# Triangular inverses in a hybrid encoder: 8 by 8 blocks solved on VectorE in place of the first three doubling levels, and a new order of the pieces around them

## The reference, cut to what matters

```python
a_mat = jnp.where(strict, einsum('bnhid,bnhjd->bnhij', kb, kc) * decay, 0.0)
unit_lower = a_mat + jnp.eye(C)
u = solve(unit_lower, vb)                      # DeltaNet, 8 heads of 128
# RWKV-7, 8 heads of 64, token by token:
sa = einsum('bhij,bhj->bhi', state, a_t)
state = state * w_t[:, :, None, :] + sa[..., None] * b_t[:, :, None, :] + v_t[..., None] * k_t[:, :, None, :]
y = einsum('bhij,bhj->bhi', state, r_t)
```

## Time and profile before

| | us |
|---|---|
| median of 3 runs | 2767.75 (2765.85 to 2768.54) |
| the profiled execution, its own time | 2771.26 |
| its span | 2769.4 |
| TensorE busy in the span | 2725.2 (98%) |
| VectorE busy | 1542.8 (56%) |
| ScalarE busy | 1312.0 (47%) |
| GpSimd busy | 119.9 (4%) |
| TensorE's mean granted clock, share of full speed | 0.997 |

### The profile page before, as it was taken

The page is one execution under the profiler, slowest core; times in us unless marked ns, Lnnn a source line. Parts: engine busy times, 40 slices in busy tenths (PEclk is TensorE's granted clock), DMA queues, the critical chain, the costliest instruction groups (busy, mean ns, idle before and its releaser), DMA issues.

```text
span 2769.4 us, 44546 instructions
## 1 busy us (share of the span) xinstructions
PE 2725.2 (98%) x18174; PEld 2393.0 (86%) x18174; DVE 1542.8 (56%) x2048; ACT 1312.0 (47%) x1798; POOL 119.9 (4%) x167
## 2 busy tenths in 40 slices
PE   8999999999999999999999999999999999999999
PEld 8999998888888888888898997888888888888887
DVE  5655466666555555555544665666665555455454
ACT  4544444555544535445444354335555444354453
POOL 0000043000000000000000000530000000000000
PEclk9999999999999999999999999999999999999999
DMA  7454500543555555555545562004445545555553
GB/s 281 181 184 159 182 33 32 213 172 143 184 201 184 190 191 189 190 183 186 193 175 201 188 220 95 2 2 160 175 140 195 192 173 197 183 191 191 183 194 140
DMA packets 67801, 461.71 MB, mean 167 GB/s; under 512 B 7023, under 2 KB 10223, under 8 KB 13084
## 3 DMA queue, kind: packets, MB, share of 16 engines
q1 hardware_dynamic: 63824, 449.47, 45.3%
q10 hardware_dynamic: 3500, 5.21, 0.6%
q0 software_dynamic: 288, 4.19, 0.4%
HBM read 456.73 MB, written 5.27 MB: 167 GB/s over the span
## 4 chain that ended last, share of the span: by engine, by line
PE 94%; DVE 3%; ACT 2%; issue 1%; DMA 0%; POOL 0%; DVEq 0%; ACTq 0%; POOLq 0%
PE bank L423 17%; PE bank L402 13%; PE bank L404 13%; PE bank L403 13%; PE bank L425 9%; PE bank L446 6%; PE bank L448 6%; PE bank L447 6%; PE bank L1199 1%; PE bank L1172 1%; PE bank L337 1%; PE bank L2477 1%; PE bank L561 0%; PE bank L505 0%; DVE split_lo L353 0%
## 5 line engine op out<-in xcount | busy, mean ns | idle before, releaser
L353 DVE TENSOR_TENSOR split_lo<-raw,split_hi 128x1024 fp32r<-128x1024 f32 x840 | 1019.9, 1224 | 943.1 <-ACT split_hi L346 942.7
L346 ACT ACTIVATE split_hi<-raw 128x1024 fp32r<-128x1024 f32 x840 | 881.4, 1059 | 1137.6 <-PE bank L404 554.9
L423 PE MATMUL bank<-hT,split_hi 128*128 128x512 f32 x2048 | 720.8, 397 | 5.4 <-issue 5.3
L425 PE MATMUL bank<-hT,split_lo 128*128 128x256 f32 x2048 | 574.4, 280 | 0.0
L423 PEld LDWEIGHTS bank<-hT,split_hi 128*128 128x128 f32 x2048 | 385.0, 188 | 93.4 <-DVE split_lo L353 1.1
L402 PE MATMUL bank<-split_hi,u_hi 128*128 128x512 f32 x1152 | 449.8, 390 | 0.0
L404 PE MATMUL bank<-split_hi,u_lo 128*128 128x512 f32 x1152 | 448.5, 389 | 0.0
L403 PE MATMUL bank<-split_lo,u_hi 128*128 128x512 f32 x1152 | 448.4, 389 | 0.0
L425 PEld LDWEIGHTS bank<-hT,split_lo 128*128 128x128 f32 x2048 | 387.4, 189 | 5.7 <-issue 5.6
L446 PE MATMUL bank<-hT,split_hi 128*128 128x256 f32 x1328 | 376.8, 284 | 0.0
L448 PE MATMUL bank<-hT,split_lo 128*128 128x256 f32 x1328 | 375.8, 283 | 0.0
(11 more groups left out here) (471 smaller groups left out, 2266.4 us busy)
## 6 DMA issues: line engine op xcount, KB each, us to landing
raw<-in_stream SPq DMA_DIRECT2D x420, 1024.0 KB, 4.8
work<-in_mem POOLq DMA_DIRECT2D x2, 2048.0 KB, 8.5
bias_rows<-bias_line SPq DMA_DIRECT2D x1, 3072.0 KB, 12.9
x<-in_x SPq DMA_DIRECT2D x1, 2048.0 KB, 9.0
out<-x SPq DMA_DIRECT2D x4, 512.0 KB, 4.9
mwork<-bias_rows ACTq DMA_DIRECT2D x1, 1536.0 KB, 11.2
work<-bias_rows ACTq DMA_DIRECT2D x1, 1536.0 KB, 10.1
rwork<-in_wide ACTq DMA_DIRECT2D x1, 1280.0 KB, 5.9
```

The lines of the kernel that those rows point to most:

```text
L346: nc.scalar.activation(split_hi[:, u % SPLIT], raw[:, b % RAW, (u % 2) * UNIT:(u % 2 + 1) * UNIT], ACT.Copy).then_inc(s_hi, 1)
L353: nc.vector.tensor_tensor(split_lo[:, u % SPLIT], raw[:, b % RAW, (u % 2) * UNIT:(u % 2 + 1) * UNIT], f32(split_hi[:, u % SPLIT]), SUB).th ...
L423: nc.tensor.matmul(out[:, :], lhsT=w_hi[:, cols], rhs=hT[:, k].rearrange("p two s -> p (two s)"), start=k == 0, stop=False)
L425: m = nc.tensor.matmul(out[:, S:2 * S], lhsT=w_lo[:, cols], rhs=hT_hi[:, k, :], start=False, stop=k == KD - 1)
```

## The change

Levels 0 to 2 go (`BASE` = 3, `TINY` = 8). The 8x8 diagonal blocks are instead inverted by forward substitution on VectorE, all at once along the free axis:

```diff
+        def dve_inv_blocks(dve, group, views, d):
+            T, Tt = views[0][:, d], views[1][:, d]
+            if group >= 2 and d == 0:
+                dve.wait_ge(iv_f, group - 1)
+            dve.wait_ge(iv_a, 2 * group + d + 1)
+            own = const[:, C["blocks"]].unsqueeze(1).broadcast_to([P, 4, HALF])
+            dve_step(nc.vector.tensor_tensor(Tt, iv_diag[:, d], own, MULT))
+            dve_step(nc.vector.reduce_sum(tiny[:, 0, d], blocks_of(Tt).rearrange("p m b c -> p m c b"), AX_X))
...
+            nc.vector.tensor_tensor(blocks_of(T), got.broadcast_to(shape), unit.broadcast_to(shape), MULT).then_inc(iv_blk, 1)
+
+        def pe_inv_around(pe, group, views):
+            pe.wait_ge(iv_blk, 2 * group + 2)
+            if group < 4:
+                pe.wait_ge(s_eg, 2 * group + 2)
+            nc.tensor.matmul(rep_bank(group)[:, :], lhsT=const[:, C["around"]],
+                             rhs=views[0].rearrange("p d m n -> p (d m n)"), start=True, stop=True).then_inc(iv_rep, 1)
+
+        def dve_inv_solve(dve, group, views):
...
+            dve.wait_ge(iv_rep, group + 1)
+            nc.vector.tensor_copy(row[:, :, 0:1], unit[:, :, 0:1])
+            dve_step(nc.vector.scalar_tensor_tensor(out=row[:, :, 1:], in0=N[:, :, 0, 1:], scalar=const[:, C["unit_neg"]],
+                                                    in1=unit[:, :, 1:], op0=MULT, op1=ADD))
+            for k in range(1, TINY - 1):
+                left = TINY - 1 - k
+                dve_step(nc.vector.tensor_tensor(part[:, :, 0:left], N[:, :, k, k + 1:],
+                                                 row[:, :, k:k + 1].broadcast_to([P, 8, left]), MULT))
+                dve_step(nc.vector.tensor_tensor(row[:, :, k + 1:], row[:, :, k + 1:], part[:, :, 0:left], SUB))
...
+            for d, (solved, turned) in enumerate(((Tt, T), (T, Tt))):
+                nc.vector.tensor_tensor(blocks_of(solved[:, d]), own, tiny[:, 1, d].unsqueeze(2).broadcast_to([P, 4, TINY, TINY]),
+                                        MULT).then_inc(iv_tt, 1)
+                dve.wait_ge(iv_tt, 8 * group + 2 * d + 1)
+                nc.vector.transpose(flat(turned[:, d]), flat(solved[:, d])).then_inc(iv_tt, 1)
```

Each `dve_step` waits until the instruction has ended. `N` lies in PSUM, `row` and `part` in SBUF. A group now has 16 TensorE slots (4 x (level - 3) + 0 to 3) and 8 slots on ScalarE and VectorE, and three GpSimd masks a direction in place of six. The slot tables and the fillers:

```diff
-                    if slot in (20, 23):
-                        pe.wait_ge(s_D, min(2 * hp + 4, 2 * DN_GROUPS))
-                        pe_fill(bank[7], 4 if slot == 20 else 5)
-        DN_PE = {'tail': (0, 1, 3, 7, 9), 'cum': (0, 13), 'mask': (2, 13), 'kk': (0,), 'kq': (10,)}
-        DN_ACT = {'tail': (0, 1, 3), 'pre': (1, 7), 'diag': (9, 11)}
-        DN_DVE = {'R': 1, 'out': 3, 'squares': 5, 'QKT': (5, 8), 'AT': (7, 9), 'first': (9, 11)}
+        DN_PE = {'tail': (0, 2, 4, 7, 10), 'cum': (15, 2), 'mask': (15, 2), 'kk': (15,), 'kq': (6,), 'around': 8}
+        DN_ACT = {'tail': (0, 1, 3), 'pre': (7, 1), 'diag': (1, 2), 'squares': 4}
+        DN_DVE = {'AT': (0, 1), 'blocks': (2, 2), 'R': 1, 'solve': 3, 'out': 5, 'QKT': (6, 7)}
-            pe.wait_ge(s_rMAT, 1)
-            pe_fill(bank[0], 16)
+            pe_rwkv_cum(pe, 1)
+            pe_inv_around(pe, 4, rw_inv[0])
+            pe_fill(bank[3], 36)
-                        pe_fill(bank[0], 7 if slot == 3 else 10)
-                    if slot == 20 or (f and slot == 23):
-                        pe_fill(bank[0], 4 if slot == 20 else 7)
+                        pe_fill(bank[0], 7)
-        RW_PE = {'tail': (0, 1, 4, 8, 9, 10), 'cum': 0, 'pairs': (15, 21)}
-        RW_ACT = {'tail': (0, 0, 1, 4, 5), 'pre': (1, 4), 'diag': (9, 11)}
-        RW_DVE = {'state': 1, 'out': 4, 'mean': 5, 'variance': 8, 'scales': 9, 'pre': (4, 5), 'pairs': (7, 7, 9, 9), 'first': (9, 11)}
-        RW_FIRST = {'keys': (1, 3, 3), 'bonus': (5, 11), 'bonus PE': 23}
+        RW_PE = {'tail': (0, 2, 4, 6, 7, 9), 'cum': 15, 'first': 5, 'around': 8, 'pairs': (11, 14)}
+        RW_ACT = {'tail': (0, 0, 1, 2, 3), 'pre': (0, 1), 'diag': (3, 3)}
+        RW_DVE = {'pre': (0, 1), 'state': 1, 'scales': 1, 'first': 2, 'blocks': 3, 'solve': 3, 'out': 4, 'pairs': (5, 7),
+                  'mean': 5, 'variance': 6}
+        RW_FIRST = {'keys': (0, 1, 1), 'bonus': (3, 7), 'bonus PE': 13}
```

- In DeltaNet, cum, mask and kk for d = 0 are made two groups ahead, in slot 15 (for group 1 before group 0, right after `ev_sc`). For group 0, `around` stands inside the last chunk of `ev_sc`:

```diff
+            elif (c, u) == (5, 4):
+                pe_inv_around(pe, 0, dn_inv[0])
```

More of the change, by code:

```diff
@@ L105 @@
 CONST_COLS = [
-    ("ident", P), ("level", 2 * (LEVELS - 1) * (P // 2)), ("eye", P // 2),
+    ("ident", P), ("level", 2 * (LEVELS - 1 - BASE) * (P // 2)),
+    ("blocks", P // 2), ("around", P), ("unit", TINY), ("unit_neg", 1),
     ("neg", 2 * P), ("cum_mid", 4 * P), ("causal", 4 * P), ("halves", P), ("ones", 1), ("half_cols", 2),
@@ L1209, in pe_inv @@
                 pe.wait_ge(s_eg, 2)
-            for level in range(1, LEVELS):
+            for level in range(BASE, LEVELS):
                 pe_inv_level(pe, group, views, AT, level, between)
@@ L1362, in pe_even @@
                 Gemm(pe, "ev_sc").column_chunk(c, after_unit=lambda u, c=c: pe_delta_head(pe, c, u))
+            for piece in ("cum", "mask", "kk"):
+                pe_delta_pre(pe, 1, 0, piece)
             for hp in range(DN_GROUPS):
                 def between(slot):
+                    if hp + 1 < DN_GROUPS and slot == DN_PE["around"]:
+                        pe_inv_around(pe, hp + 1, dn_inv[(hp + 1) % 2])
                     for step in range(5):
@@ L1479, in pe_delta_pre @@
                                          stop=piece == "cum" or i == 1)
[L1480 removed]
+                if piece == "mask":
+                    m.then_inc(s_mask, 1)
                 return
@@ L2575, in between @@
                 def between(slot):
+                    for d in range(2):
+                        if f + 1 < RW_F and slot == RW_ACT["pre"][d]:
+                            act_rwkv_pre(act, f + 1, d)
                     for step in range(5):
@@ L2950, in constants @@
     own, t_ = s % half, np.arange(half)[None, :]
-    level = np.zeros((P, 2, LEVELS - 1, half), np.float32)
-    for n_, size in enumerate(1 << np.arange(LEVELS - 1)):
+    level = np.zeros((P, 2, LEVELS - 1 - BASE, half), np.float32)
+    for n_, size in enumerate(1 << np.arange(BASE, LEVELS - 1)):
         pair = (own // (2 * size)) == (t_ // (2 * size))
@@ L2956, in constants @@
     c[:, at["level"]] = level.reshape(P, -1)
-    c[:, at["eye"]] = own == t_
+    c[:, at["blocks"]] = own // TINY == t_ // TINY
+    c[:, at["around"]] = s // TINY == t // TINY
+    c[:, at["unit"]] = s % TINY == np.arange(TINY)[None, :]
+    c[:, at["unit_neg"]] = -1.0 * (s % TINY == 0)
     c[:, at["neg"]] = np.where(np.hstack([s <= t, s >= t]), 0.0, NEG)
```

408 lines of the change are left out of this document (255 added, 153 removed).

## The result

| | before | after |
|---|---|---|
| median, us | 2768.14 (2765.85 to 2768.73, 4 runs) | 2819.47 (2807.77 to 2829.26, 4 runs) |
| ratio to before | | 1.0185, 95% interval 1.014 to 1.0231 |
| the profiled execution, its own time | 2771.26 | 2825.84 |
| its span | 2769.4 | 2824.1 |
| TensorE's mean granted clock | 0.997 | 0.975 |

What follows compares the result with a forecast made beforehand. TensorE, busy for 98% of the span, was taken as the bound, with new waits for VectorE. DeltaNet -6.8, RWKV +7.8 and clock +7 gave +8.0 us, moving the median 2767.75 to 2776; range 2752 to 2792.

Steps and rivals of the forecast that it cites:

- Clock: Half-speed TensorE work after waits, ten waits over 2 us counted: +7 us, bounds 0 and 14.
- Fillers: Filler matmuls at 0.24 us each leaving TensorE in DeltaNet and RWKV groups, counted as time saved: -19 us.
- TensorE stays full: Rival, whole kernel: no new wait arises, so all work taken off TensorE is gained: -42 us, near 2727; chance 0.05.
- (d): DeltaNet group 1: the tail just covers a 4.7 us solve, masks may lengthen it: 23.7 to 26.6, taken 25.4 us.
- (j): RWKV group 5: 26.4 us of work plus waits at around and behind GpSimd: 30.4 to 34.6, taken 32.8 us.
- (k): RWKV group 6, without cum: 31.0 us.
- (a): DeltaNet group 0's around, near 352 in the GEMM: TensorE waits 3.2 to 4.9 us for VectorE, taken 4.4, plus 0.9.
- (b): Group 1's cum, mask and kk now before DeltaNet's group 0: +2.6 us, so its level 3 starts at 368.5.
- (c): DeltaNet group 0: 14.4 us of TensorE work with no tail to hide waits: 22.0 us (20.9 to 22.5).
- (g): DeltaNet's last tail: 10.6 us plus 1.0 for squares and a split ahead of its first copy, 11.6 in the sum.
- (i): RWKV group 4: VectorE's queue sets its length, 41.4 us against 21.0, the largest single term, +20 us (39.5 to 42.2).
- waits as summed, clock holds: Rival, whole kernel: DeltaNet -6.8 and RWKV +7.8 without clock loss give +1, about 2768 us; chance 0.20.

Runs made afterwards that it cites:

- e1: The changed kernel with fillers put into three RWKV waits of groups 4 to 6 (before first, around and cum): 2808.1 us, ratio 1.0145.
- e12: The changed kernel with GpSimd's long products behind group 7's masks, bonus and group 0's around later, fillers in DeltaNet and RWKV waits: 2798.31 us.
- e7: The changed kernel with the solve's 14 small instructions issued twice in all eight groups: 2845.76 us, ratio 1.0278.
- e4: The kernel before, without 37 fillers of slots 20 and 23 in the four RWKV groups: 2768.58 us, ratio 1.0008.
- e9: DeltaNet from the changed kernel with group 0's around two units later and fillers in its waits, RWKV from the kernel before: 2759.4 us, ratio 0.9965.
- e10: The changed kernel with GpSimd's four long products all behind group 7's masks, none in groups 5 and 6: 2813.22 us, ratio 1.0163.
- e6: The changed kernel with fillers in DeltaNet's and RWKV's waits, group 0's around two units later and the bonus one slot later: 2799.95 us, ratio 1.011.
- e2: The changed kernel with group 0's around called two units later, after unit 6 in place of unit 4: 2822.25 us, ratio 1.02.

## Why the prediction was wrong

**The sign of the forecast was right, its size not**: +8 against +51. The part that failed is **Clock**.

- **Clock, the term that was mis-sized.** "Most half-speed work will lie beside a VectorE that is late anyway" is the sentence that failed; I gave 7 us, bounds 0 and 14. Half-speed time rose from 17 to 141 us, and each of it cost 0.47 us by the spread of the runs: 58 us. In groups 4, 5 and 6 alone (1 - PEclk) x length is 11.5 + 20.2 + 19.1 = 51 us. A part of that is time in which TensorE stood still; taken over its busy time alone, in stretches of 1 us, it is at most 43 us in these groups and 59 in the whole execution, against 8 in the kernel before. By these counts the clock is of the size of the loss. What experiments gave back is less: 28 us in groups 5 and 6 (e1), and 21 us of the 51 in the median (e12), where half of the half speed was still there. That the rest is clock too rests on the slope and on this count. e7 shows the error from the other side: in RWKV a longer solve still fits beside TensorE's half-speed work. The reason is in the row at 1840: the clock did not come back when the wait was over. It stayed at 1.2 GHz through the tail's last step, level 5 and the pairs, work that lies on the path. I had read rows 9 as a price for one wait and not asked what a group with three such waits does.
- **Fillers, -19 us in the sum.** Wrong by e4 for the 8.9 us that it tried: those of RWKV's last slots were worth nothing, since they stood in waits. DeltaNet's were not tried. Only the 2729 of "TensorE stays full" rested on all of it, but (d), (f), (j) and (l) took their share too, and (e) and (k) through them.
- **(a), (b)** `around` near 352: the trace has the wait of 5.36 us, above my 3.2 to 4.9, and level 3 at 372.9 in place of 368.5. The rest is clock again, products at half speed until the GEMM's end (0.81 in the first row above).
- **(c)** 25.4 us against 22.0. Its waits were 1.7, 1.9 and 0.8, and its clock 0.66.
- **(d)** 23.5 against 25.4, under my lower bound of 23.7. The solve took 4.8 us, the lower of my two values (4.7). The masks did come, but not beside it. Group 1, VectorE's timeline (the blocks' first reduction, the solve's first and last small instruction, its last transpose), then GpSimd's:

```profile
408.26 0.62 DVE L1261 TENSOR_REDUCE tiny<-work 128x32 f32<-128x256 f32 x1
...
412.22 0.17 DVE L1284 COPY tiny<-const 128x8 f32<-128x8 f32 x1 [0.54 <-PE bank L1273]
...
415.07 0.17 DVE L1291 TENSOR_TENSOR tiny<-tiny 128x8 f32<-128x8 f32 x1
...
416.53 0.45 DVE L1298 STREAM_TRANSPOSE work<-work 128x256 f32<-128x256 f32 x1
```
```profile
410.68 1.58 POOL L1170 TENSOR_TENSOR work<-iv_diag,const 128x256 f32<-128x256 f32 x2
416.65 1.42 POOL L2009 TENSOR_TENSOR hwork<-work 128x256 f32<-128x256 f32 x2 [4.39 <-PE bank L1601]
```

  GpSimd stood still from 412.3 to 416.65 since it waited for the tail's last step; I had it wait for the fourth alone. The reduction took 0.62 us where I had taken a transpose's 0.45.
- **(e), (f), (g)** 21.6, 20.5 and 13.2 against 23.3, 19.0 and 11.6; of (g) the clock of 0.78 could be the whole difference of 1.6 (0.22 x 13.2 = 2.9 at most). In sum DeltaNet was forecast at -6.8 and came to +0.4; with the clock held (e9) to -4.1, inside my bounds.
- **(h)** 1756.9 against 1756.6: right.
- **(i)** 49.95 against 41.4. The bonus took 1.59 + 3.41 us in place of 1.18 + 1.67, as GpSimd's masks now ran beside it; and I missed that `cum` waits for the last masked pairs, 2.6 us. The rest is clock.
- **(j), (k)** 54.6 and 48.9 against 32.8 and 31.0. In group 5 the excess of 21.8 is 17.2 us more of TensorE busy (43.6 for 26.4) and 4.5 more of waits (10.9 for 6.4): `cum` again, 2.5, and `first`, whose factor products stood behind GpSimd.
- **(l), (m)** together 43.1 against 38.8, with up to 0.24 x 17.7 = 4.2 us of clock in the tail.

The rival "waits as summed, clock holds" gave 2768; by the runs' own slope the change would stand at 2758 there. Of these 10 us 5.9 are by the traces the shorter GEMMs behind RWKV, which the sum did not have. So the accounting of what was added and removed was near, if the extrapolation holds; it was not near part by part, as the misses in (i) to (k) show. Of the signs named in advance, three came: the wait near 352 (5.4 us, for 3 to 5), the solve near 4.7, low clock in more than two stretches. P6a waiting 3 us for the solve did not (0.8 at most), and group 4 took 50 us with VectorE 63% busy, not 41 with over 75%. The sign of being wrong that I had named for groups 1 and 2, "come near 22 us", came for group 2 (21.6), yet not for the reason given: the solve cost what the 128x1 product suggests, and its cover held.

What stays open: why the clock comes back early in one execution and late in the next. The same kernel spent 107 to 153 us at half speed, and no experiment here controls that.

## What to carry to other kernels

Where waits of several microseconds enter a stage of short products, look at the granted clock before costing anything: in group 5 the clock was at half from 1818 to 1855, behind waits of 2.8 and 4.9 us, and TensorE was busy for 24.4 of the 30 us from 1820 on. That loss, up to 12 us there, fell on work that had been on the path all along. Fillers that stand in a wait are no saving, and putting some into a new wait is the first test of whether the wait or the clock is the loss. Look for what a moved piece now stands beside: GpSimd's long products left one place on VectorE's path and landed on the solve (e10, e12). Judge a large change by stages: here one of them was harmless and, with its clock held, worth having.

## What the runs showed of the hardware

- The granted clock stayed at 0.50 for ten microseconds in which TensorE was busy throughout (the row at 1840), and fell to 0.52 in a stretch behind a single wait of 0.75 us (e6). The Trainium skill (TensorE: Matmul & The Clock Gate, "What's actually happening") says that activity releases the throttle and that idleness brings it back. The row at 1840 does not go with the first half, e6's not with the second, if activity is what these rows call busy. Which kind of work counts as activity is not told by any run here.
- A VectorE product with two SBUF operands took 2.13 and 2.56 us beside GpSimd's of 1.90 and 2.40 us, against 0.38 alone, and a solve instruction of 128x16 took 0.50 us beside GpSimd's product of 128x256 (e2) against 0.17. In e10 the solve's updates, both operands in SBUF, took 2.01 to 2.15 us beside products of 2.35 us, while the multiplications between them, one operand in PSUM, kept their 0.19 to 0.21. The Trainium skill (SBUF — State Buffer, "SBUF: two separate sides") has it as an exclusive lock for a whole instruction; by that rule the traces agree.
- Small dependent VectorE instructions cost little: 0.20 to 0.25 us from start to start for 128x8 to 128x48 (the solves of the changed kernel). The blocks' reduction, 128x256 to 128x32, took 0.61 to 0.62 us, a product of 128x256 0.38 to 0.42.
- Half the clock did not double the time of short products: a record of 64x32 took 1.6 times as long at 1.2 GHz (3.63 us for 64 against 1.12 for 32).
